# Routed experts: blocks numbered expert by expert, one fetch of each weight, a block table in registers, a split float32r down product

## The chip, the cores and the metric

One core of a Trainium2 chip runs the whole kernel. The metric is the device time of one execution in microseconds. The kernel before was run three times: median 1275.41 us, lowest 1274.18, highest 1277.51. A further execution was recorded by the hardware profiler.

## The reference

One layer of an encoder on 1024 tokens of width 1024: RMSNorm, one combined input projection, attention and a gated convolution in parallel, an output projection, and then a mixture of experts. The change touches only the last:

```
x = x + HierMoE(rms_norm(x, g_ffn))
# per token: the group of 8 experts with the highest logit, in it the two best experts
a = h @ w_e_gate[e];  u = h @ w_e_up[e]        # 1024 x 256 each, 32 experts
mid = silu(a) * u * weight(token, e)
x += mid @ w_e_down[e]                          # 256 x 1024
```

All of it is float32. An expert has 3 MB of weights, gate, up and down with 1 MB each. Each token goes to two experts, so 2048 rows are spread over 32 experts.

## The kernel before

Each engine has its own program (`block.sync` for SyncE's queue, `block.gpsimd`, `block.scalar` for ACT, `block.vector`, `block.tensor`), and semaphores tie them together. The stages are the input projection, attention, the two branches with their merge, the output projection with routing, and the expert stage.

Routing gives every (token, expert) pair a place in a list of blocks of 128 rows. Each of the 32 experts has a home block with its own number (`home`), and rows past the 128th go into overflow blocks from number 32 on (`shift`, `over`, lines 1113 to 1122). `bexp` says which expert an overflow block belongs to, and `ntrip_i` how many groups of four there are, at least one (lines 1174 to 1181).

The expert stage runs over the blocks in groups of four (`SLOTS`), a hardware loop over groups and an unrolled body of four on every engine, and the last group behind the loop. A matrix product in full float32 precision is done as three float32r products (`three`, line 1219): the high part times the high part, low times high, high times low. The high part is a copy into a float32r tile, the low part is the difference of the two.

For a block, by engine:

- SyncE, `load_expert` (line 408): waits until the gate and up products of the block four before are done (`gu_ps`), issues gate and up weights into `wgu_raw`, waits for that block's down product (`y_ps`), issues `wed`. The overflow blocks load their expert's weights again, with the expert's number read from `bexp` into a register (lines 439 to 443).
- GpSimd: `gather` (line 531) fetches 128 rows by an indirect DMA into `hg`, five blocks ahead; `scatter` (line 539) adds the block's output rows to the result in DRAM by an indirect DMA and waits for the scatter before it to have landed (`y_out`).
- ACT, `act_block` (line 788): silu of the block, the high half of the weights of the block after the next in two pieces (`expert_hi`, 128x2048 each, lines 769 to 771), between them the high part of its gathered rows (`gathered_hi`), then the left half of the output (line 799).
- VectorE, `dve_block` (line 1191): silu times up (`mid`), the copy of the transposed product (`midT`), the low halves of the weights (`expert_lo`, line 1163, written over the raw tile) around the low part of the gathered rows (`gathered_lo`), the row indices and weights of the block (`rcol`, `wcol`), the right half of the output (line 1206).
- TensorE, `pe_block` (line 1506): half the gate and up product of the next block, transposes of `mid`, transposes of the gathered rows of the block after it, the other half, then `down` (lines 1495 to 1504): four float32 matmuls of 512 columns, two instructions each in the trace.

## Time and profile before

| | |
|---|---|
| median of three runs | 1275.41 us |
| profiled execution, whole | 1278.19 us |
| its span, first to last instruction | 1276.2 us |
| TensorE busy | 1171.4 us, 92% |
| VectorE busy | 756.7 us, 59% |
| ACT busy | 468.3 us, 37% |
| GpSimd busy | 199.4 us, 16% |
| expert weights fetched | 36 x 3 loads of 1024 KB |
| moved by all DMA | 172.26 MB, of it 16.81 MB by the indirect ones of GpSimd |
| expert stage, first weight load issued to the end | 817.3 to 1276.2 us |

Times in the rows are microseconds from the first instruction unless marked ns, and in rows a number in square brackets is the idle time of the engine before the instruction, with what ended it. L1163 is line 1163 of the kernel. PE is TensorE, PEld its weight loads, DVE VectorE, POOL GpSimd, SP SyncE, and a q behind a name its instruction queue. Matmul instructions overlap, so what one costs is the distance between two starts, and not the length shown.

### The profile page before, as it was taken

What the parts mean: (1) busy time and instruction counts of PE and PEld (TensorE: products, weight loads), DVE (VectorE), ACT (ScalarE), POOL (GpSimd) and SP (SyncE); (2) the same over time, 40 slices, a digit from 0 to 9 for tenths busy, and PEclk for the clock granted to TensorE, in tenths of its full rate; (3) what the DMA queues carried; (4) which work ended last, traced back from release to release, by engine and by line L of the source; (5) the groups of instructions that cost most, each with busy time, mean ns of one, the idle gap of its engine ahead of it and who ended that gap; (6) DMA issues with size and microseconds to landing.
All of it is one profiled execution on the core that took longest, in us unless ns stands there. A gap on an engine that the chain in (4) does not pass through costs nothing.

```text
span 1276.2 us, 14857 instructions
## 1 busy us (share of the span) xinstructions
PE 1171.4 (92%) x5388; PEld 891.4 (70%) x5388; DVE 756.7 (59%) x992; ACT 468.3 (37%) x635; POOL 199.4 (16%) x243
## 2 busy tenths in 40 slices
PE   4999999999878999999999899859999889889996
PEld 4988888886645576776778788746676656666664
DVE  4448999983424454544465334476777556556663
ACT  4522111113533444444232111124555544554552
POOL 4010000000232332120000000011222221222121
PEclk9999999999969999999799899858999999999999
DMA  6021111111000000000410323495999999999980
GB/s 224 1 66 33 49 49 49 50 50 34 24 1 1 1 1 1 1 17 18 164 56 11 96 107 132 171 318 165 327 337 319 305 323 313 343 328 311 313 279 9
DMA packets 101541, 172.26 MB, mean 135 GB/s; under 512 B 11727, under 2 KB 45690, under 8 KB 101498
## 3 DMA queue, kind: packets, MB, share of 16 engines
q1 hardware_dynamic: 91002, 154.86, 35.8%
q0 software_dynamic: 10432, 16.81, 5.5%
q8 instruction: 26, 0.43, 0.1%
q14 instruction: 17, 0.14, 0.0%
q10 hardware_dynamic: 64, 0.02, 0.0%
HBM read 165.35 MB, written 27.26 MB: 151 GB/s over the span
## 4 chain that ended last, share of the span: by engine, by line
PE 67%; DMA 13%; DVE 6%; ACT 5%; issue 5%; SPq 2%; POOL 2%; ACTq 0%; DVEq 0%; POOLq 0%
PE pb L1221 14%; PE pb L1223 14%; PE pb L1222 14%; DMA wgu_raw<-in_w_e_up 11%; PE pb L1503 5%; PE pb L1361 4%; PE pb L1338 4%; PE pb L1350 2%; PE pb L1270 2%; PE pb L1475 2%; PE pb L1280 1%; SPq L417 1%; PE pb L1421 1%; DMA ws_raw<-in_w_conv_out 1%; ACT wgu_hi L771 1%
## 5 line engine op out<-in xcount | busy, mean ns | idle before, releaser
L1163 DVE TENSOR_TENSOR wgu_lo<-wgu_raw,wgu_hi 128x2048 fp32r<-128x2048 f32 x72 | 164.6, 2287 | 63.5 <-ACT wgu_hi L771 63.4
L771 ACT ACTIVATE wgu_hi<-wgu_raw 128x2048 fp32r<-128x2048 f32 x72 | 137.1, 1908 | 56.5 <-DMA wgu_raw<-in_w_e_up 56.5
L871 DVE SCALAR_TENSOR_TENSOR cv<-up,dwc,cv 128x1024 f32<-128x1024 f32 x120 | 154.1, 1284 | 3.7
L1221 PE MATMUL pb<-hT_hi,ws_hi 128*128 128x512 f32 x384 | 151.7, 395 | 0.0
L1223 PE MATMUL pb<-hT_hi,ws_lo 128*128 128x512 f32 x384 | 149.5, 389 | 0.0
L1222 PE MATMUL pb<-hT_lo,ws_hi 128*128 128x512 f32 x384 | 149.5, 389 | 0.0
L1221 PE MATMUL pb<-wgu_hi,hgT_hi 128*128 128x512 f32 x288 | 128.2, 445 | 6.3 <-DVE hgT_lo L1170 6.1
L1503 PE MATMUL pb<-wed,midT 128*128 128x512 f32 x288 | 129.5, 592 | 0.5 <-DVE midT L1196 0.5
L1223 PE MATMUL pb<-wgu_hi,hgT_lo 128*128 128x512 f32 x288 | 113.7, 395 | 0.0
L1222 PE MATMUL pb<-wgu_lo,hgT_hi 128*128 128x512 f32 x288 | 113.3, 393 | 0.0
L1503 PEld LDWEIGHTS pb<-wed,midT 128*128 128x128 f32 x288 | 54.4, 189 | 55.2 <-issue 51.8
L694 ACT ACTIVATE pr<-pb,nmax 128x128 f32<-128x128 f32 (+7 forms) x64 | 47.4, 741 | 112.6 <-DVE nmax L989 112.6
L1221 PEld LDWEIGHTS pb<-hT_hi,ws_hi 128*128 128x128 f32 x384 | 72.1, 188 | 15.9 <-issue 1.0
L1222 PEld LDWEIGHTS pb<-hT_lo,ws_hi 128*128 128x128 f32 x384 | 72.1, 188 | 15.9 <-issue 1.0
L1361 PEld LDWEIGHTS pb<-vv,pT 128*128 128x128 f32 x576 | 73.1, 197 | 14.3 <-DVE pT L1005 7.5
L1223 PEld LDWEIGHTS pb<-hT_hi,ws_lo 128*128 128x128 f32 x384 | 72.1, 188 | 15.2
L1361 PE MATMUL pb<-vv,pT 128*128 128x64 f32 x576 | 75.4, 277 | 6.9 <-DVE pT L1005 6.3
L548 POOL DMA_INDIRECT out<-yb,rcol x36 | 57.4, 1595 | 151.5 <-issue 102.6
L1221 PEld LDWEIGHTS pb<-wgu_hi,hgT_hi 128*128 128x128 f32 x288 | 55.7, 193 | 28.9 <-issue 19.2
L1338 PE MATMUL pb<-kT,qT 96*128 96x512 f32 (+3 forms) x192 | 75.0, 500 | 0.5 <-DVE kT L938 0.5
L1005 DVE COPY pT<-pb 128x512 f32<-128x512 f32 (+3 forms) x64 | 37.7, 589 | 60.5 <-PE pb L1350 60.2
L799 ACT ACTIVATE yb<-pb,wcol 128x512 f32<-128x512 f32 x36 | 24.8, 690 | 125.8 <-DVE wcol L1203 67.8
(281 smaller groups left out, 2017.8 us busy)
## 6 DMA issues: line engine op xcount, KB each, us to landing
wgu_raw<-in_w_e_gate SPq DMA_DIRECT2D x36, 1024.0 KB, 11.2
wgu_raw<-in_w_e_up SPq DMA_DIRECT2D x36, 1024.0 KB, 20.6
wed<-in_w_e_down SPq DMA_DIRECT2D x36, 1024.0 KB, 18.4
ws_raw<-in_w_in SPq DMA_DIRECT2D x24, 512.0 KB, 3.8
xs<-in_x SPq DMA_DIRECT2D x8, 512.0 KB, 8.7
wout<-in_w_out SPq DMA_DIRECT2D x1, 4096.0 KB, 12.8
xb<-in_x SPq DMA_DIRECT2D x8, 512.0 KB, 5.2
h_rows<-h SPq DMA_DIRECT2D x8, 512.0 KB, 2.6
```

Source lines behind the costliest of these rows:

```text
L548: g.indirect_dma_start(out=out[0], out_offset=bass.IndirectOffsetOnAxis(ap=rcol[b][:, 0:1].bitcast(U32), axis=0), in_=yb[b][:, :], in_offs ...
L694: a.activation(pr[:, n % 2, 0:w], banks(2 * (n % 2), 2)[:, 0:w], ACT.Exp, bias=nmax[:, n % 2:n % 2 + 1], accum_out=rsum[:, j % 2, h:h + 1] ...
L771: a.activation(wgu_hi[q % 2][:, :, ks, :], wgu_raw[q % SLOTS][:, :, ks, :], ACT.Copy).then_inc(gu_hi, 1)
L871: i = v.scalar_tensor_tensor(out=cv[:, c, :], in0=src, scalar=w, in1=cv[:, c, :], op0=ALU.mult, op1=ALU.add)
L1005: v.tensor_copy(pT[:, m % 2, 0:min(512, (j + 1) * P)], banks(4, 1)[:, 0:min(512, (j + 1) * P)]).then_inc(pt_d, 1)
L1163: v.tensor_tensor(wgu_lo[q % SLOTS][:, :, ks, :], wgu_raw[q % SLOTS][:, :, ks, :], wgu_hi[q % 2][:, :, ks, :].bitcast(F32), ALU.subtract). ...
L1221: t_.matmul(out, w(0), m(0), start=start, stop=False)
L1222: t_.matmul(out, w(0), m(1), start=False, stop=False)
L1223: return t_.matmul(out, w(1), m(0), start=False, stop=stop)
L1338: t_.matmul(S[:, f:e], qT[0:QK, j % 2, h * P:(h + 1) * P], kT[0:QK, h, f:e], start=True, stop=(e < w))
L1361: i = t_.matmul(pb[:, 6, h * VD:(h + 1) * VD], pT[:, n % 2, k * P:(k + 1) * P], vv[:, k, h * VD:(h + 1) * VD], start=(k == 0), stop=(k == j))
L1503: m = t_.matmul(pb[:, 4 + h, :], midT[:, f, :], wed[q][:, f, h * 512:(h + 1) * 512], start=(f == 0), stop=(f == 1))
```

## The change

- Blocks are numbered expert by expert: the blocks of expert 0, then those of expert 1, and so on, at least one each. The total is rounded up to a multiple of four.
- SyncE's program no longer has loops: it fetches each expert's weights once, in order, gate and up into one of four places of `wgu_raw`, down into one of three places of `wed_raw`. It waits for a register's value of `gu_lo` and `dn2_lo` (`landed_by`: twice the number of blocks up to that expert) before it fills a place again, and counts landed weights in `gu_here` and `down_here`, in program order.
- A table `btab_i` holds for each block its expert's number plus one, the place of its gate and up weights, and the place of its down weights. VectorE computes it, TensorE turns it into one row, and ACT, VectorE and GpSimd read its entries into registers.
- The low halves of gate and up weights have two tiles of their own, so that the raw tile stays.
- The down product is split in the same way as the gate and up product, 12 float32r matmuls a block: ACT copies the high part of the down weights (`down_hi`, two halves of 128x1024), GpSimd subtracts for the low part (`down_lo`), VectorE splits `midT`.
- ACT and VectorE do their steps in a new order: silu and `mid` of the next block come before the output of this one, and the first half of the weights is split three blocks ahead.

```diff
 SLOTS = 4
+DSLOTS = 3
 NBT = MAXB + SLOTS
+NTAB = 64
 GLU_UNITS = 2 * NC
 GATE_UNITS = 2 * D // P
...
-    WO = [R2 + 24 * K * i for i in range(SLOTS)]
-    wgu_raw = [place(f"wgu_raw{i}", [P, 2, KD, FF], F32, o) for i, o in enumerate(WO)]
-    wgu_lo = [place(f"wgu_lo{i}", [P, 2, KD, FF], F32R, o) for i, o in enumerate(WO)]
+    wgu_raw = place("wgu_raw", [P, SLOTS, 2, KD, FF], F32, R2)
+    wed_raw = place("wed_raw", [P, DSLOTS, 2, D], F32, R3)
     wgu_hi = [place(f"wgu_hi{i}", [P, 2, KD, FF], F32R, R1 + 16 * K * i) for i in range(2)]
-    wed = [place(f"wed{i}", [P, 2, D], F32, o + 16 * K) for i, o in enumerate(WO)]
+    wgu_lo = [place(f"wgu_lo{i}", [P, 2, KD, FF], F32R, o) for i, o in enumerate((R1 + 32 * K, R6 + 8 * K))]
+    wed_hi = place("wed_hi", [P, 2, D], F32R, R6)
+    wed_lo = place("wed_lo", [P, 2, D], F32R, R3 + 24 * K)
...
+    sil = place("sil", [P, FF], F32, ONO)
+    mid = place("mid", [P, FF], F32, ONO + K)
+    midT = [place(f"midT_{n}", [P, 2, P], F32R, QDO + 8 * K + K * s) for s, n in enumerate(("hi", "lo"))]
...
+            pair = "(o p i) f -> p o (i f)"
+            def load_gu(e):
+                b = e % SLOTS
+                sp.dma_start(wgu_raw[:, b, 0, :, :].rearrange("p (o i) f -> p o (i f)", i=2), w_e_gate[0, e].rearrange(pair, p=P, i=2)).then_inc(w_in0[b], 16)
+                sp.dma_start(wgu_raw[:, b, 1, :, :].rearrange("p (o i) f -> p o (i f)", i=2), w_e_up[0, e].rearrange(pair, p=P, i=2)).then_inc(w_in0[b], 16)
+            def load_down(e):
+                b = e % DSLOTS
+                sp.dma_start(wed_raw[:, b, :, :], w_e_down[0, e].rearrange("(k p) f -> p k f", p=P)).then_inc(w_in1[b], 16)
+            def confirm_gu(e):
+                sp.wait_ge(w_in0[e % SLOTS], 32 * (e // SLOTS + 1))
+                sp.sem_inc(gu_here, 1)
+            def confirm_down(e):
+                sp.wait_ge(w_in1[e % DSLOTS], 16 * (e // DSLOTS + 1))
+                sp.sem_inc(down_here, 1)
...
-                    load_expert(0, 0, None)
+                    load_gu(0)
...
+            for e in range(1, SLOTS):
+                load_gu(e)
+                load_down(e - 1)
+            confirm_gu(0)
             sp.wait_ge(bexp_ok, 1)
...
-                    load_expert(q, e, i * SLOTS + (q + 1 + NE - SLOTS))
+            for e in range(SLOTS, NE + 2):
+                confirm_gu(e - 3)
+                if e >= SLOTS + 1:
+                    confirm_down(e - SLOTS - 1)
+                if e < NE:
+                    split = sp.value_load(landed_by[0:1, e - SLOTS:e - SLOTS + 1], min_val=2, max_val=2 * MAXB)
+                    sp.wait_ge(gu_lo, split)
+                    load_gu(e)
+                if e >= SLOTS + 1:
+                    split = sp.value_load(landed_by[0:1, e - SLOTS - 1:e - SLOTS], min_val=2, max_val=2 * MAXB)
+                    sp.wait_ge(dn2_lo, split)
+                    load_down(e - 2)
+            confirm_gu(NE - 1)
+            for e in range(NE - 3, NE):
+                confirm_down(e)
             sp.wait_ge(y_all, 2)
...
+            def table(col):
+                return btab_i[0:1, bass.ds(col, 1)]
+            def down_lo(q, i):
+                s = pool.value_load(table(i * SLOTS + (q + 2 * NTAB)), min_val=0, max_val=DSLOTS - 1)
+                for h in range(2):
+                    pool.wait_ge(dn2_hi, i * (2 * SLOTS) + (2 * q + h + 1))
+                    g.tensor_tensor(wed_lo[:, h, :], wed_raw[:, bass.ds(s, 1), h, :].rearrange("p o f -> p (o f)"), wed_hi[:, h, :].bitcast(F32), ALU.subtract).then_inc(dn2_lo, 1)
...
+            down_lo(0, 0)
             with pool.Fori(0, last) as i:
                 for q in range(SLOTS):
                     gather(q % 2, i * SLOTS + (q + SLOTS + 1))
+                    down_lo(q + 1, i)
                     scatter(q % 2, i * SLOTS + (q + 1), i * (8 * SLOTS) + 16 * ((q + 1) // 2 + 1))
             for q in range(SLOTS):
+                if q < SLOTS - 1:
+                    down_lo(q + 1, last)
                 scatter(q % 2, last * SLOTS + (q + 1), last * (8 * SLOTS) + 16 * ((q + 1) // 2 + 1))
...
+            def expert_hi(q, h, s):
                 ks = slice(h * (KD // 2), (h + 1) * (KD // 2))
-                a.activation(wgu_hi[q % 2][:, :, ks, :], wgu_raw[q % SLOTS][:, :, ks, :], ACT.Copy).then_inc(gu_hi, 1)
+                raw = wgu_raw[:, 0, :, ks, :] if s is None else wgu_raw[:, bass.ds(s, 1), :, ks, :].rearrange("p o g k f -> p (o g) k f")
+                a.activation(wgu_hi[q % 2][:, :, ks, :], raw, ACT.Copy).then_inc(gu_hi, 1)
+            def place_of(q, i):
+                return act.value_load(table(i * SLOTS + (q + NTAB)), min_val=0, max_val=SLOTS - 1)
+            def first_half(q, i):
+                e = act.value_load(table(i * SLOTS + q), min_val=1, max_val=NE)
+                s = place_of(q, i)
+                act.wait_ge(gu_here, e)
+                expert_hi(q, 0, s)
+            def down_hi(q, i):
+                e = act.value_load(table(i * SLOTS + q), min_val=1, max_val=NE)
+                s = act.value_load(table(i * SLOTS + (q + 2 * NTAB)), min_val=0, max_val=DSLOTS - 1)
+                act.wait_ge(down_here, e)
+                act.wait_ge(y_ps, i * SLOTS + (q + 1))
+                for h in range(2):
+                    a.activation(wed_hi[:, h, :], wed_raw[:, bass.ds(s, 1), h, :].rearrange("p o f -> p (o f)"), ACT.Copy).then_inc(dn2_hi, 1)
+            def silu(q, i):
+                nth = i * SLOTS + (q + 1)
+                act.wait_ge(gu_ps, nth)
+                a.activation(sil[:, :], pb[:, GU_BANK[q % 2], 0:FF], ACT.Silu).then_inc(sil_ok, 1)
...
+            act.wait_ge(gu_here, 1)
+            expert_hi(0, 0, None)
+            expert_hi(0, 1, None)
             act.wait_ge(bexp_ok, 1)
-            last = act.value_load(ntrip_i[0:1, 1:2], min_val=NE // SLOTS, max_val=MAXB // SLOTS - 1)
-
-            def act_block(q, i, more):
+            first_half(1, 0)
+            gathered_hi(0, 1)
+            expert_hi(1, 1, place_of(1, 0))
+            gathered_hi(1, 2)
+            last = act.value_load(ntrip_i[0:1, 0:1], min_val=NE // SLOTS - 1, max_val=MAXB // SLOTS - 1)
+            act.wait_ge(swt_ps, 1)
...
+            def act_block(q, i, left):
                 nth = i * SLOTS + (q + 1)
-                act.wait_ge(gu_ps, nth)
-                a.activation(sil[:, :], pb[:, GU_BANK[q % 2], 0:FF], ACT.Silu).then_inc(sil_ok, 1)
-                if more:
-                    act.wait_ge(w_in0[(q + 2) % SLOTS], (i + (q + 2) // SLOTS) * 32 + 32)
-                    expert_hi(q + 2, 0)
+                if left > 2:
+                    expert_hi(q + 2, 1, place_of(q + 2, i))
                     gathered_hi(q, i * SLOTS + (q + 3))
-                    expert_hi(q + 2, 1)
-                act.wait_ge(y_ps, nth)
+                if left > 1:
+                    silu(q + 1, i)
+                if left > 3:
+                    first_half(q + 3, i)
+                if left > 1:
+                    down_hi(q + 1, i)
+                act.wait_ge(y_ps, nth + 1)
                 act.wait_ge(wc_ok, nth)
                 a.activation(yb[q % 2][:, 0:512], pb[:, 4, :], ACT.Copy, scale=wcol[q % 2][:, :]).then_inc(y_a, 1)
+            silu(0, 0)
+            first_half(2, 0)
+            down_hi(0, 0)
             with act.Fori(0, last) as i:
                 for q in range(SLOTS):
-                    act_block(q, i, True)
+                    act_block(q, i, SLOTS)
             for q in range(SLOTS):
-                act_block(q, last, q < SLOTS - 2)
+                act_block(q, last, SLOTS - q)
...
-            link(v.tensor_scalar(shift[:, :], shift[:, :], float(P), float((NE - 1) * P), ALU.mult, ALU.add))
-            link(v.tensor_tensor(shift[:, :], shift[:, :], home[:, :], ALU.subtract))
-            v.tensor_tensor(rank[:, :, :], ranks, row(home[:, :], NE), ALU.add)
-            link(v.scalar_tensor_tensor(out=over[:, :, :], in0=ranks, scalar=float(P), in1=row(shift[:, :], NE), op0=ALU.is_ge, op1=ALU.mult))
-            link(v.tensor_tensor(rank[:, :, :], rank[:, :, :], over[:, :, :], ALU.add))
+            link(v.scalar_tensor_tensor(out=shift[:, :], in0=shift[:, :], scalar=float(P), in1=home[:, :], op0=ALU.mult, op1=ALU.add))
+            link(v.tensor_tensor(rank[:, :, :], ranks, row(shift[:, :], NE), ALU.add))
...
+            link(v.tensor_tensor(incl[:, :], incl[:, :], up32[:, :], ALU.add))
+            link(v.tensor_scalar(bcmp[:, :], incl[:, :], pcol[:, 0:1], None, ALU.is_le))
+            link(v.reduce_sum(be_f[:, 0:1], bcmp[:, :], axis=AX.X))
+            link(v.tensor_scalar(be_f[:, 1:2], be_f[:, 0:1], float(NE - 1), None, ALU.min))
+            link(v.tensor_copy(be_i[:, 0:1], be_f[:, 1:2]))
+            v.tensor_scalar(btab[:, 0:1], be_f[:, 1:2], 1.0, None, ALU.add)
+            v.tensor_scalar(cmp3[:, :], io3[:, :], be_f[:, 1:2], None, ALU.is_le)
+            link(v.tensor_single_scalar(be_i[:, 1:2], be_i[:, 0:1], SLOTS - 1, op=ALU.bitwise_and))
+            link(v.reduce_sum(be_f[:, 0:1], cmp3[:, :], axis=AX.X))
+            v.tensor_copy(btab[:, 1:2], be_i[:, 1:2])
+            v.scalar_tensor_tensor(out=btab[:, 2:3], in0=be_f[:, 0:1], scalar=-float(DSLOTS), in1=be_f[:, 1:2], op0=ALU.mult, op1=ALU.add).then_inc(btab_ok, 1)
+            v.tensor_scalar(landed_by[:, :], incl[0:1, :], 2.0, None, ALU.mult)
+            link(v.tensor_scalar(cmp4[:, :], io4[:, :], incl[0:1, NE - 1:NE], None, ALU.is_lt))
+            link(v.reduce_sum(ntrip_f[:, :], cmp4[:, :], axis=AX.X))
+            v.tensor_scalar(ntrip_i[:, :], ntrip_f[:, :], -1.0, None, ALU.add)
...
-            def expert_lo(q, h, halves):
+            dve.wait_ge(btab_ps, 1)
+            v.tensor_copy(btab_i[:, :], pb[0:1, 5, 0:3 * NTAB]).then_inc(bexp_ok, 1)
+            def table(col):
+                return btab_i[0:1, bass.ds(col, 1)]
+            def expert_lo(q, h, i):
                 ks = slice(h * (KD // 2), (h + 1) * (KD // 2))
-                dve.wait_ge(gu_hi, halves)
-                v.tensor_tensor(wgu_lo[q % SLOTS][:, :, ks, :], wgu_raw[q % SLOTS][:, :, ks, :], wgu_hi[q % 2][:, :, ks, :].bitcast(F32), ALU.subtract).then_inc(gu_lo, 1)
+                s = dve.value_load(table(i * SLOTS + (q + NTAB)), min_val=0, max_val=SLOTS - 1)
+                dve.wait_ge(gu_hi, i * (2 * SLOTS) + (2 * q + h + 1))
+                v.tensor_tensor(wgu_lo[q % 2][:, :, ks, :], wgu_raw[:, bass.ds(s, 1), :, ks, :].rearrange("p o g k f -> p (o g) k f"), wgu_hi[q % 2][:, :, ks, :].bitcast(F32), ALU.subtract).then_inc(gu_lo, 1)
...
-            expert_lo(0, 0, 1)
-            expert_lo(0, 1, 2)
...
+            for i in range(2):
+                dve.wait_ge(h2_out[i], 16 * NTILE // 2)
+            dve.wait_ge(bexp_ok, 1)
+            last = dve.value_load(ntrip_i[0:1, 0:1], min_val=NE // SLOTS - 1, max_val=MAXB // SLOTS - 1)
+            expert_lo(0, 0, 0)
+            expert_lo(0, 1, 0)
             dve.wait_ge(swt_ps, 1)
...
+            expert_lo(1, 1, 0)
+            def middle(q, i):
+                nth = i * SLOTS + (q + 1)
+                dve.wait_ge(sil_ok, nth)
...
+            def dve_block(q, i, left):
                 b, nth = q % 2, i * SLOTS + (q + 1)
-                dve.wait_ge(sil_ok, nth)
-                v.tensor_tensor(mid[:, :], sil[:, :], pb[:, GU_BANK[b], FF:2 * FF], ALU.mult).then_inc(mid_ok, 1)
+                m = pb[:, 3, 0:FF].rearrange("p (f t) -> p f t", f=2)
                 dve.wait_ge(mt_ps, nth)
-                v.tensor_copy(midT[:, :, :], pb[:, 3, 0:FF].rearrange("p (f t) -> p f t", f=2)).then_inc(mt_ok, 1)
-                if more:
-                    expert_lo(q + 2, 0, i * (2 * SLOTS) + (2 * q + 5))
+                v.tensor_copy(midT[0][:, :, :], m).then_inc(mt_hi, 1)
+                dve.wait_ge(mt_hi, nth)
+                v.tensor_tensor(midT[1][:, :, :], m, midT[0][:, :, :].bitcast(F32), ALU.subtract).then_inc(mt_ok, 1)
+                if left > 2:
+                    expert_lo(q + 2, 1, i)
                     gathered_lo(b, i * SLOTS + (q + 3), i * SLOTS + (q + SLOTS))
-                    expert_lo(q + 2, 1, i * (2 * SLOTS) + (2 * q + 6))
+                if left > 1:
+                    middle(q + 1, i)
                 dve.wait_ge(y_out[b], i * (8 * SLOTS) + 16 * (q // 2 + 1))
                 v.tensor_scalar(rcol[b][:, :], stok[:, bass.ds(i * SLOTS + q, 1)], 0.0, None, ALU.add)
                 v.tensor_scalar(wcol[b][:, :], swt[:, bass.ds(i * SLOTS + q, 1)], 1.0, None, ALU.mult).then_inc(wc_ok, 1)
+                if left > 3:
+                    expert_lo(q + 3, 0, i)
                 dve.wait_ge(wc_ok, nth)
-                dve.wait_ge(y_ps, nth)
+                dve.wait_ge(y_ps, nth + 1)
                 v.tensor_scalar(yb[b][:, 512:1024], pb[:, 5, :], wcol[b][:, :], None, ALU.mult).then_inc(y_d_ok, 1)
+            middle(0, 0)
+            expert_lo(2, 0, 0)
             with dve.Fori(0, last) as i:
                 for q in range(SLOTS):
-                    dve_block(q, i, True)
+                    dve_block(q, i, SLOTS)
             for q in range(SLOTS):
-                dve_block(q, last, q < SLOTS - 2)
+                dve_block(q, last, SLOTS - q)
...
+            pe.wait_ge(btab_ok, 1)
+            for c in range(3):
+                i = t_.matmul(pb[0:1, 5, c * NTAB:(c + 1) * NTAB], btab[:, c:c + 1], ident[:, 0:NTAB], start=True, stop=True)
+            i.then_inc(btab_ps, 1)
...
+            pe.sem_inc(y_ps, 1)
...
-                    m = three(pb[:, GU_BANK[q % 2], :], lambda s: hgT[q % 2][s][:, k, :], lambda s: (wgu_lo[q % SLOTS] if s else wgu_hi[q % 2])[:, :, k, :], k == 0, k == KD - 1)
+                    m = three(pb[:, GU_BANK[q % 2], :], lambda s: hgT[q % 2][s][:, k, :], lambda s: (wgu_lo if s else wgu_hi)[q % 2][:, :, k, :], k == 0, k == KD - 1)
...
-                pe.wait_ge(w_in1[q], i * 16 + 16)
+                pe.wait_ge(dn2_lo, i * (2 * SLOTS) + (2 * q + 2))
...
-                        m = t_.matmul(pb[:, 4 + h, :], midT[:, f, :], wed[q][:, f, h * 512:(h + 1) * 512], start=(f == 0), stop=(f == 1))
+                        m = three(pb[:, 4 + h, :], lambda s: midT[s][:, f, :], lambda s: (wed_lo if s else wed_hi)[:, f, h * 512:(h + 1) * 512], f == 0, f == 1)
```

## Rows read from the trace of the kernel before

**Rows 1.** The page's part 1: busy us by engine (share of the span) x instructions

```profile
PE 1171.4 (92%) x5388; PEld 891.4 (70%) x5388; DVE 756.7 (59%) x992; ACT 468.3 (37%) x635; POOL 199.4 (16%) x243
```

**Rows 2.** Stages: length, PE, PEld, DVE, ACT, POOL busy, clock, DMA share, GB/s

```profile
935.00:955.00 20.00, 20.00 (x85) 14.17 (x84) 14.73 (x18) 11.19 (x10) 5.27 (x4) 1.00 0.99 330
1050.00:1100.00 50.00, 44.73 (x177) 31.18 (x178) 30.42 (x38) 25.19 (x22) 11.78 (x9) 0.95 0.99 327
1100.00:1150.00 50.00, 46.50 (x187) 32.34 (x187) 31.71 (x37) 26.44 (x24) 10.55 (x8) 0.98 1.02 330
```

**Rows 3.** The chain of waits, early blocks: start, us, what

```profile
881.32 3.43 PE pb L1503 x8
...
891.43 3.43 PE pb L1503 x8
```

**Rows 4.** The same chain, later blocks

```profile
1056.14 3.45 PE pb L1503 x8
...
1067.09 20.52 DMA wgu_raw<-in_w_e_up
...
1096.19 1.28 ACT L791
...
1104.07 3.45 PE pb L1503 x8
```

**Rows 5.** The same chain, the end

```profile
1261.89 0.69 ACT yb L799
...
1264.32 3.71 PE pb L1503 x8
...
1269.90 1.55 POOL out L548
```

**Rows 6.** Groups of instructions, 850 to 1276: busy us, mean ns, idle before

```profile
L1163 DVE TENSOR_TENSOR wgu_lo<-wgu_raw,wgu_hi 128x2048 fp32r<-128x2048 f32 x72 | 164.6, 2287 | 63.5 <-ACT wgu_hi L771 63.4
L771 ACT ACTIVATE wgu_hi<-wgu_raw 128x2048 fp32r<-128x2048 f32 x68 | 129.8, 1908 | 56.5 <-DMA wgu_raw<-in_w_e_up 56.5
...
L1170 DVE TENSOR_TENSOR hgT_lo<-pb,hgT_hi 128x1024 fp32r<-128x1024 f32 x36 | 43.7, 1215 | 1.8 <-ACT hgT_hi L775 1.8
...
L1196 DVE COPY midT<-pb 128x256 f32<-128x256 f32 x36 | 15.3, 424 | 34.4 <-PE pb L1492 34.4
```

**Rows 7.** DMA issues: KB each, median us from issue to landing

```profile
wgu_raw<-in_w_e_up SPq DMA_DIRECT2D x36, 1024.0 KB, 20.6
```

**Rows 8.** TensorE in order of time, gate-up products

```profile
919.73 0.40 PE L1223 MATMUL pb<-wgu_hi,hgT_lo 128*128 128x512 f32 x1
919.96 0.40 PE L1221 MATMUL pb<-wgu_hi,hgT_hi 128*128 128x512 f32 x1
```

**Rows 9.** SyncE's queue in order of time

```profile
884.78 0.37 SPq L417 DMA_DIRECT2D wed<-in_w_e_down  x1
...
1163.02 4.76 SPq L417 DMA_DIRECT2D wed<-in_w_e_down  x1
1168.03 3.74 SPq L413 DMA_DIRECT2D wgu_raw<-in_w_e_gate  x1
...
1210.02 3.41 SPq L417 DMA_DIRECT2D wed<-in_w_e_down  x1
...
1214.35 2.10 SPq L413 DMA_DIRECT2D wgu_raw<-in_w_e_gate  x1
```

**Rows 10.** VectorE and GpSimd in order of time, first 60 us

```profile
18.79 2.33 DVE L856 TENSOR_TENSOR wdn_lo<-wdn_raw,wdn_hi 128x2080 fp32r<-128x2080 f32 x1 [1.64 <-ACT wdn_hi L603]
...
18.84 4.96 POOL L493 TENSOR_TENSOR wdn_lo<-wdn_raw,wdn_hi 128x1248 fp32r<-128x1248 f32 x1 [3.98 <-ACT wdn_hi L603]
23.88 0.19 POOL L485 TENSOR_SCALAR rs<-ss 128x1 f32<-128x1 f32 x1
...
24.79 0.75 POOL L485 TENSOR_SCALAR rs<-ss 128x1 f32<-128x1 f32 x1
```

**Rows 11.** VectorE in order of time, the wait for the slot product

```profile
852.91 0.21 DVE L1154 TENSOR_SCALAR stok<-pb 128x52 int32<-128x52 f32 x1 [3.04 <-PE pb L1457]
```

80 lines of the change are left out of this document (27 added, 53 removed).

## The prediction

> **What bounds the kernel now.** Read the engine totals first [rows 1]: TensorE is 92% busy over the span, but that is an average. The change touches only the expert stage, the last third, so I read the busy times by stage next [rows 2]. At 935 to 955 TensorE is busy without a gap and the DMA share is already 0.99; at 1050 to 1150 TensorE drops to 44.7 and 46.5 of 50 us while the DMA share stays at 0.99 and 1.02. The chain shows both regimes. Early, it is pure TensorE work and a block costs 10.12 us (the down products start at 881.32 and 891.43) [rows 3]. Later it is issue by SyncE, 20.52 us of landing, then ACT and VectorE halves, and four blocks cost 47.93 us, 11.98 each (1056.14 to 1104.07) [rows 4]. Over the stage, first down end to last down end is 884.75 to 1268.03, 383.3 us for 35 intervals, 10.95 each [rows 3, 5]. So two things hold the stage: TensorE at 10.1 us a block, and weight traffic of 36 x 3 MB.
>
> The other engines have room now. Scaled from 20 us at 935 to 955 to a block of 10.12 us, VectorE is busy 14.73 / 20 x 10.12 = 7.5 us a block, of it 2 x 2.29 with the weights' low halves and 1.21 with the gathered rows'; ACT 11.19 gives 5.7 us, of it 2 x 1.91 with the high halves; GpSimd, which only issues a gather and a scatter, 5.27 gives 2.7 us [rows 2, 6].
>
> **The change part by part.**
> Number of blocks: counted from the reference's router on these inputs, experts 18, 19, 20 and 22 of the 32 get 129 to 256 rows and all others 1 to 128, so 32 + 4 = 36 blocks, as the trace has: 36 loads of each weight [rows 6, 7]. Rounded up to a multiple of four it is 36 before and after. Nothing is gained in blocks.
>
> DMA: 36 x 3 MB become 32 x 3 MB, 12.6 MB less; at the 330 GB/s of the saturated stretches [rows 2] that is 38 us of DMA time. It is worth that only where DMA is the bound. The after kernel also frees a raw slot when VectorE has taken its low half, not when TensorE has used it, so a load starts earlier than before by about 2 blocks less the 12.5 us at which the low half is done, some 8 us. With the four overflow blocks in the middle (blocks 19 to 26), where no load is needed, I take DMA to be off the path from there on. In the first 18 blocks it needs 3.15 MB of weights + some 0.4 MB of rows per block over 0.33 MB/us = 10.8 us.
>
> Down products: 8 instructions in 3.43 us [rows 3] become 12 of the gate-up's form, which follow each other at 0.23 us [rows 8]: 2.74 us, 0.69 us less. TensorE then needs 10.12 - 0.69 = 9.43 us a block.
>
> ACT: adds two copies of 128x1024, half of the 1.91 us of 128x2048 each [rows 6], 1.9 us: 7.6 us. It also reads registers: SyncE's gap between two issues is 0.25 us in the loop without a read (1163.02 + 4.76 to 1168.03) and 0.92 us with one (1210.02 + 3.41 to 1214.35) [rows 9], so 0.67 us each. Of ACT's five reads a block two stand behind the short silu and cost about 1.1 us, the others lie under running copies. That makes 8.7 us, still under 9.4. VectorE: one more 128x256, 0.42 us as the `midT` copy [rows 6]: 7.9 us.
>
> GpSimd: the new low halves of 128x1024. The only row of this form is 128x1248 in 4.96 us, started together with VectorE's 2.33 us on the same two tiles, one engine's instruction held by the other's: 4.96 - 2.33 = 2.63 us for 1248, so 2.15 us for 1024; one short GpSimd form tells the same, 0.75 us where it meets a running VectorE instruction and 0.19 where not [rows 10]. Bounds for one half: 1.15 us (VectorE's 2.29 for 2048 halved; the ring below falls to 8.8 and TensorE's 9.43 holds) and 4.1 us (4.96 scaled, always held). I take 2.15 when free, the value of its own row less the hold, and price the hold by the order of work; 4.1 would count it twice, so it sets no end of the range. GpSimd's sum is 4.3 + 2.7 = 7.0 us. The Trainium skill, "SBUF — State Buffer", section "Who interferes with whom", speaks against this part: a VectorE instruction with two SBUF inputs and a GpSimd one that reads SBUF exclude each other for their whole length, whichever began first. The trace shows GpSimd waiting for VectorE; no row shows VectorE waiting for GpSimd. By the rule the forecast below stands; without it the first rival.
>
> So I price the exclusion in both directions. No engine's sum exceeds 9.4 us, but the order does. From the end of gate-up n+1 (time 0): silu to 0.6, reads, ACT's first high half of n+3 from 1.65 to 3.55, the two down copies to 5.45, output copy, second high half to 8.0. VectorE's low half of n+3 runs 3.6 to 5.85 and holds off GpSimd, which takes 5.85 to 8.0; at 8.0 VectorE's next low half and GpSimd's second become ready together. If GpSimd is first, the ring is VectorE half 2.29, gathered low half 1.21, `mid` 0.42, the two short column instructions 0.3, GpSimd half 2.15, VectorE half 2.29, GpSimd half 2.15: 10.8 us a block. If VectorE is first, the down product starts at 12.6 and the next one on time, (12.6 + 9.43) / 2 = 11.0. I take 10.8.
>
> New wait on SyncE: weights e are reported as landed (gu_here) only after the down load of e is issued, which waits for the down low half of e-3. Behind that wait are queued the report, ACT's high half of e, and behind it the down copies of e-2: a ring of 1.9 + 2.3 + 2.15 + 2.15 + 0.3 = 8.8 us plus the issue. An issue takes 0.37 us with an empty queue and 3 to 4 us with a full one [rows 9]. At 10.8 us a block the queue is not full for long, so I price it at nothing; its cover is the 2.0 us between 8.8 and 10.8.
>
> Start: the table takes 15 small VectorE instructions of some 0.2 us, 3 us, ahead of the wait for the slot product, in which VectorE sat idle for 3.04 us [rows 11]; three longer ones ahead of it and eight behind it go. If that cover were gone, the stage would begin 3 us later. The first low halves come as before. The first down product must wait for copies and two GpSimd halves behind the third block's low half: 3 us later, end 887.7 instead of 884.7. End: the last block's down copies and GpSimd halves follow the down product before, 1.0 + 4.3 + 0.3 + 2.9 = 8.5 us instead of the present 6.1 (1261.9 to 1268.0), then 8.1 us as now [rows 5].
>
> Sum: 887.7 + 34 x 10.8 + 8.5 + 8.1 = 1271.5 us of span. The profiled execution had a span of 1276.2 and 1278.19 us in all, the median of the runs is 1275.41, 0.8 under the span. So 1271 us.
>
> **The rivals.**
> 1. The exclusion works only against GpSimd, or costs little. Then GpSimd's halves overlap VectorE's and a block costs 9.4 to 10.0; the first 18 stay at DMA's 10.6. 887.7 + 18 x 10.6 + 16 x 9.9 + 16.6 = 1253.5; with 9.43 in the second part 1246. For it: no row shows VectorE held. Against it: the two tiles' reads that hold GpSimd are the same.
> 2. Slower: the report behind the down load. From an issue time of 2.0 us on, SyncE's ring exceeds 10.8; at 3.5 us it is 12.3. In the 18 blocks where DMA is nearly full that is + 27 us: 1298. For it: the share of 0.99 already at 10.1 us a block, and landings of 20.6 us [rows 2, 7]. Against it: 12.6 MB less, and earlier loads.
> 3. Slower: reads and ties fall badly (each read on ACT's path over 1 us, VectorE first at most ties, ACT's table load of 1.28 us each fourth block [rows 4]): 11.4 us, 1271 + 34 x 0.6 = 1291.
> 4. The loads aren't saved: only if an expert were empty or the count differed; the 36 blocks speak against it. It would read as 36 loads and some 1290.
>
> **How the numbers follow.** Forecast 0.40 (1262 to 1280, from 10.55 to 11.05 a block); rival 1 0.26; rival 2 0.20; rival 3 0.12; rival 4 0.02. Within 0.3% (about what a measurement of this kernel can tell from no change) is 1271.6 to 1279.2. Faster: rival 1 and 0.21 of the forecast, 0.47. Same: 0.13 of the forecast and 0.02 of the others, 0.15. Slower: 0.38. The forecast alone straddles the line. Range 1240 to 1303: below, rival 1 with 9.43; above, rival 2 with a margin for its 18 blocks becoming 20.
>
> **What would show it.** 32 loads of each weight. Down products of 12 at 0.23 us. GpSimd's halves near 2.15 us where VectorE is idle and up to 4.4 beside it; VectorE's 2.29 us stretched in turn (mean over 2.6) is the exclusion, unchanged 2.29 is rival 1. Down starts 10.8 us apart. TensorE's waits moved from landings to the down low half and hgT_lo. ACT's high half waiting for SyncE after a long down issue is rival 2. The prediction is wrong if the distance of the down starts is under 10.4 or over 11.2.

## The result and the profile after

The kernel after the change takes 1310.47 us (median of four runs, 1310.02 to 1314.04); the kernel before, on the same chip, 1275.96. The ratio is 1.0277, with a 95% interval of 1.0254 to 1.0300: slower by 2.8%. The forecast was 1271 us and its range ended at 1303. The profiled execution has a span of 1307.7 us and took 1310.24 us. Ratios here and below are of undisturbed executions: one of the four of experiment 7 took 2347.45 us, nearly double, is left out of its ratio, and why it did so is open.

Two lines of the page of the kernel after: the engine totals and the loads of the up weights (median us to landing at the end). They answer to [rows 1, 7].

```profile
PE 1165.0 (89%) x5538; PEld 923.2 (71%) x5538; DVE 833.6 (64%) x1034; ACT 531.0 (41%) x701; POOL 468.4 (36%) x319
...
wgu_raw<-in_w_e_up SPq DMA_DIRECT2D x32, 1024.0 KB, 11.8
```

Two engines changed out of proportion. GpSimd went from 199 to 468 us, and VectorE gained 77 us although only some 36 x 0.42 us, 15 us, of work of its own was added in the blocks. The loads are 32 instead of 36 and land in 11.8 us, where they took 20.6.

Stages of the kernel after: length, then busy us of PE, PEld, DVE, ACT and POOL, granted clock, DMA share, GB/s [rows 2].

```profile
880.00:1050.00 170.00, 147.45 (x647) 117.93 (x646) 121.15 (x144) 107.80 (x100) 140.67 (x57) 0.92 0.83 283
1050.00:1240.00 190.00, 161.63 (x748) 125.66 (x748) 173.04 (x163) 124.77 (x114) 173.08 (x66) 1.00 0.78 251
```

TensorE is busy for 87 and 85%, also where the DMA share is only 0.78. The transfers no longer set the pace there; in the second stretch VectorE and GpSimd are both at 91%.

Groups of the kernel after, 850 us to the end: busy us, mean ns of one, then the idle time before and its releasers [rows 6].

```profile
L1262 DVE TENSOR_TENSOR wgu_lo<-wgu_raw,wgu_hi 128x2048 fp32r<-128x2048 f32 x72 | 232.0, 3224 | 52.8 <-ACT wgu_hi L820 50.5 <-issue 1.8
L591 POOL TENSOR_TENSOR wed_lo<-wed_raw,wed_hi 128x1024 fp32r<-128x1024 f32 x72 | 199.2, 2787 | 40.9 <-ACT wed_hi L837 40.3
L580 POOL DMA_INDIRECT out<-yb,rcol x36 | 97.0, 2693 | 19.1 <-issue 11.8 <-DMA out<-yb,rcol 6.9
L567 POOL DMA_INDIRECT hg<-h_rows,icol x36 | 70.2, 1949 | 33.5 <-issue 25.9 <-DVE icol L1267 7.6
```

The same VectorE instruction had a mean of 2287 ns before [rows 6]; it is the same instruction on the same shape and takes 0.94 us more on average. The stretching shows in a single block. GpSimd of the kernel after, in order of time (start, us, what; in brackets the idle time before):

```profile
1104.60 4.73 POOL L591 TENSOR_TENSOR wed_lo<-wed_raw,wed_hi 128x1024 fp32r<-128x1024 f32 x2
1109.49 3.47 POOL L580 DMA_INDIRECT out<-yb,rcol  x1 [0.17 <-issue]
1113.27 2.98 POOL L567 DMA_INDIRECT hg<-h_rows,icol  x1 [0.30 <-issue]
1116.27 4.74 POOL L591 TENSOR_TENSOR wed_lo<-wed_raw,wed_hi 128x1024 fp32r<-128x1024 f32 x2
```

And VectorE in the same 12 us:

```profile
1105.73 5.75 DVE L1262 TENSOR_TENSOR wgu_lo<-wgu_raw,wgu_hi 128x2048 fp32r<-128x2048 f32 x1 [0.42 <-ACT wgu_hi L820]
1111.41 0.14 DVE L1267 TENSOR_SCALAR icol<-stok 128x1 int32 x1
1111.47 1.21 DVE L1269 TENSOR_TENSOR hgT_lo<-pb,hgT_hi 128x1024 fp32r<-128x1024 f32 x1
1112.60 0.40 DVE L1287 TENSOR_TENSOR mid<-sil,pb 128x256 f32<-128x256 f32 x1
...
1113.05 2.28 DVE L1262 TENSOR_TENSOR wgu_lo<-wgu_raw,wgu_hi 128x2048 fp32r<-128x2048 f32 x1
1115.25 0.74 DVE L1308 TENSOR_SCALAR yb<-pb,wcol 128x512 f32<-128x512 f32 x1
```

Read the two side by side. VectorE's half begins at 1105.73, while GpSimd's halves run until 1109.33, and ends only at 1111.48: 2.29 us of work after a hold of 3.46. The scatter issued at 1109.49 takes 3.47 us, not 1.6: it waits for that VectorE half to end and then does its work. The gather issued at 1113.27 takes 2.98 us, not 1.04: it waits for VectorE's second half, until 1115.33. That second half itself is not held (2.28 us). So each of the two engines waits for the other in turn, and GpSimd has no idle time in this block but the gaps of 0.17 and 0.30 us. The closed ring of one block is GpSimd's halves 4.73, rest of VectorE's half 2.08, small VectorE work 1.64, second half 2.28, rest of the gather 0.92, 0.02 to the next halves: 11.67 us.

The scatter is not in this ring. In 5 of the 17 blocks between 1050 and 1240 it began 1.0 to 2.2 us late, because it waits for the scatter before it to have landed, and then took 1.60 to 2.64 us. Those blocks are 11.66 to 11.69 us long all the same, since the gather behind it is held until VectorE's second half ends. The landing of the scatters, which the chain of waits often names in this stretch, is therefore not what makes a block longer.

### The profile page after: what moved, and what is told of

Same layout as the page of the kernel before. It is cut to its first block, busy times and chain, and to the rows that moved or that the text cites. A ratio compares the mean times of both kernels' runs of the same rounds, so it can differ in the third digit from the quotient of the medians.

```text
span 1307.7 us, 16802 instructions
## 1 busy us (share of the span) xinstructions
PE 1165.0 (89%) x5538; PEld 923.2 (71%) x5538; DVE 833.6 (64%) x1034; ACT 531.0 (41%) x701; POOL 468.4 (36%) x319
## 4 chain that ended last, share of the span: by engine, by line
PE 63%; issue 9%; DVE 7%; DMA 7%; POOL 5%; ACT 5%; DVEq 1%; ACTq 1%; SPq 1%; POOLq 0%
PE pb L1325 15%; PE pb L1327 14%; PE pb L1326 14%; DMA out<-yb,rcol 6%; PE pb L1465 4%; PE pb L1442 4%; POOL wed_lo L591 3%; PE pb L1454 2%; PE pb L1374 2%; PE pb L1384 1%; DVE wgu_lo L1262 1%; PE pb L1525 1%; DVE hgT_lo L1269 1%; DMA ws_raw<-in_w_conv_out 1%; PE pb L1584 1%
## 5 line engine op out<-in xcount | busy, mean ns | idle before, releaser
L1262 DVE TENSOR_TENSOR wgu_lo<-wgu_raw,wgu_hi 128x2048 fp32r<-128x2048 f32 x72 | 232.0, 3224 | 52.8 <-ACT wgu_hi L820 50.5
L591 POOL TENSOR_TENSOR wed_lo<-wed_raw,wed_hi 128x1024 fp32r<-128x1024 f32 x72 | 199.2, 2787 | 40.9 <-ACT wed_hi L837 40.3
L820 ACT ACTIVATE wgu_hi<-wgu_raw 128x2048 fp32r (+1 forms) x72 | 137.4, 1910 | 63.1 <-SPq L432 35.3
L517 POOL TENSOR_SCALAR ssh<-ssh 128x8 f32<-128x8 f32 x16 | 3.1, 196 | 403.6 <-DVE ssh L1008 402.8
L1325 PE MATMUL pb<-wgu_hi,hgT_hi 128*128 128x512 f32 x288 | 119.8, 416 | 8.5 <-DVE hgT_lo L1269 8.5
L1325 PE MATMUL pb<-wed_hi,midT_hi 128*128 128x512 f32 x144 | 64.2, 446 | 55.0 <-issue 29.2
L517 POOL TENSOR_SCALAR rs<-ss 128x1 f32<-128x1 f32 x16 | 3.8, 236 | 284.9 <-ACT sq L804 261.5
L580 POOL DMA_INDIRECT out<-yb,rcol x36 | 97.0, 2693 | 19.1 <-issue 11.8
L837 ACT ACTIVATE wed_hi<-wed_raw 128x1024 fp32r x72 | 72.2, 1051 | 47.7 <-PE pb L1327 38.3
L1465 PEld LDWEIGHTS pb<-vv,pT 128*128 128x128 f32 x576 | 73.1, 198 | 14.3 <-DVE pT L1083 7.5
L567 POOL DMA_INDIRECT hg<-h_rows,icol x36 | 70.2, 1949 | 33.5 <-issue 25.9
## 6 DMA issues: line engine op xcount, KB each, us to landing
wgu_raw<-in_w_e_up SPq DMA_DIRECT2D x32, 1024.0 KB, 11.8
```

The source lines that it names most:

```text
L567: g.indirect_dma_start(out=hg[b][:, :], out_offset=None, in_=h2_d, in_offset=bass.IndirectOffsetOnAxis(ap=icol[b][:, 0:1].bitcast(U32), ax ...
L580: g.indirect_dma_start(out=out[0], out_offset=bass.IndirectOffsetOnAxis(ap=rcol[b][:, 0:1].bitcast(U32), axis=0), in_=yb[b][:, :], in_offs ...
L591: g.tensor_tensor(wed_lo[:, h, :], wed_raw[:, bass.ds(s, 1), h, :].rearrange("p o f -> p (o f)"), wed_hi[:, h, :].bitcast(F32), ALU.subtra ...
L820: a.activation(wgu_hi[q % 2][:, :, ks, :], raw, ACT.Copy).then_inc(gu_hi, 1)
L837: a.activation(wed_hi[:, h, :], wed_raw[:, bass.ds(s, 1), h, :].rearrange("p o f -> p (o f)"), ACT.Copy).then_inc(dn2_hi, 1)
L1262: v.tensor_tensor(wgu_lo[q % 2][:, :, ks, :], wgu_raw[:, bass.ds(s, 1), :, ks, :].rearrange("p o g k f -> p (o g) k f"), wgu_hi[q % 2][:, ...
```

## The experiments

Each ratio is against the kernel before on the same chip, whose median lay between 1277.97 and 1278.92 us in the experiments. In the expectations, X is the theory that VectorE's and GpSimd's instructions with two SBUF inputs hold each other, in both directions, and that this and GpSimd's place in the order of a block make the kernel slow. S is rival 2, the report of landed weights queued behind the down load on SyncE. A is ACT's order with its register reads. Kernel 1 is the kernel of experiment 1, and so on.

**1. Take the low half away.** GpSimd still waits and still reports, but writes eight columns instead of 1024 in all blocks but the first, so the rest of the low half is left out:

```diff
-            def down_lo(q, i):
+            def down_lo(q, i, n=8):
...
-                    g.tensor_tensor(wed_lo[:, h, :], wed_raw[:, bass.ds(s, 1), h, :]..., wed_hi[:, h, :].bitcast(F32), ALU.subtract).then_inc(dn2_lo, 1)
+                    g.tensor_tensor(wed_lo[:, h, 0:n], wed_raw[:, bass.ds(s, 1), h, 0:n]..., wed_hi[:, h, 0:n].bitcast(F32), ALU.subtract).then_inc(dn2_lo, 1)
...
-            down_lo(0, 0)
+            down_lo(0, 0, D)
```

> The kernel after, but GpSimd subtracts the low half of the down weights for block 0 only; for all later blocks its two instructions cover 8 columns of 1024, so the down product uses a stale low half (that part of the computation is left out). Theory X, the exclusion between VectorE's two-input instructions and all GpSimd instructions (subtractions, and the issues of gather and scatter, which went from 1.6 and 1.1 us to 2.7 and 1.9 on average): without 4.8 us of subtraction GpSimd is far from full, VectorE's weight halves return to about 2.3 us and a block costs 9.6 to 10.3 us instead of 11.7; time 1245 to 1265 us. Theory S, SyncE's report behind the down load: the order of waits is as before, only the low half is done earlier; 1285 to 1300. Theory A, ACT's order with its register reads: about 10.8 us a block, 1275.

Measured: 1251.89 us, ratio 0.9789 (0.9772 to 0.9806). Its groups, 850 us to the end:

```profile
L1262 DVE TENSOR_TENSOR wgu_lo<-wgu_raw,wgu_hi 128x2048 fp32r<-128x2048 f32 x72 | 165.7, 2302 | 86.0 <-ACT wgu_hi L820 83.4 <-issue 2.4
```

All other parts of the change together are worth 2.1%; the GpSimd halves alone cost some 58 us, though GpSimd had the room for them by its sum. VectorE's half is back at its old length.

**2. The same low halves on VectorE**, behind its output instruction; nothing else moved:

```diff
+            def down_lo(q, i):
+                s = dve.value_load(table(i * SLOTS + (q + 2 * NTAB)), min_val=0, max_val=DSLOTS - 1)
+                for h in range(2):
+                    dve.wait_ge(dn2_hi, i * (2 * SLOTS) + (2 * q + h + 1))
+                    v.tensor_tensor(wed_lo[:, h, :], wed_raw[:, bass.ds(s, 1), h, :]..., wed_hi[:, h, :].bitcast(F32), ALU.subtract).then_inc(dn2_lo, 1)
```

> The kernel after with the two subtractions of the down weights' low half given to VectorE, at the end of its block, all else the same. Theory X: two instructions of about 1.2 us instead of 2.4 and nothing to exclude but the two DMA issues; VectorE's sum becomes 10.3 to 10.6 us a block and it is the bound, 10.6 to 11.0 us a block; time 1268 to 1285. Theory S or A: GpSimd wasn't the cause, and VectorE now has more to do: 1305 to 1325.

Measured: 1272.11 us, ratio 0.9954 (0.9938 to 0.9971). Groups and, below, the stretch of 1130 to 1230 of this kernel:

```profile
L1252 DVE TENSOR_TENSOR wgu_lo<-wgu_raw,wgu_hi 128x2048 fp32r<-128x2048 f32 x72 | 164.7, 2289 | 29.6 <-issue 17.2 <-ACT wgu_hi L810 12.3
L1278 DVE TENSOR_TENSOR wed_lo<-wed_raw,wed_hi 128x1024 fp32r<-128x1024 f32 x72 | 84.9, 1219 | 0.7 <-ACT wed_hi L827 0.5 <-issue 0.2
```

```profile
1130.00:1230.00 100.00, 93.04 (x441) 74.83 (x440) 94.77 (x118) 70.99 (x67) 27.74 (x19) 1.00 0.83 271
```

Work given to the engine with the larger sum is 38 us cheaper than on the one with room. One half costs VectorE 1.22 us and GpSimd 2.36 free. VectorE is 95% busy in this stretch, TensorE 93%, and VectorE is the likely bound.

**3. The report ahead of the down load.**

```diff
             for e in range(SLOTS, NE + 2):
-                confirm_gu(e - 3)
...
                     load_gu(e)
+                if e - 2 < NE:
+                    confirm_gu(e - 2)
```

> The kernel after with one change in SyncE's program: the landing of gate and up weights e-2 is reported right after the load of e is issued, ahead of the wait for the down low half, instead of behind the down load. Theory X: GpSimd's instructions and their holds fill its 11.7 us; within 0.5% of the kernel after, 1304 to 1314. Theory S: ACT waited 33 us in all for this report in 15 blocks; time 1275 to 1290.

Measured: 1310.74 us, ratio 1.0254 (1.0237 to 1.0272), against 1.0277 with the report behind. Rival 2 falls: ACT's high halves waited 32.9 us in all for this report in the kernel after and not at all here, and the time is the same. SyncE's queue fits that. In the kernel after an issue takes 0.4 to 0.7 us from 850 us on, never the 3 to 5 us of [rows 9]:

```profile
910.85 0.37 SPq L428 DMA_DIRECT2D wed_raw<-in_w_e_down  x1
911.98 0.37 SPq L423 DMA_DIRECT2D wgu_raw<-in_w_e_gate  x1
912.39 0.51 SPq L424 DMA_DIRECT2D wgu_raw<-in_w_e_up  x1
```

**4. The single fetch and the new numbering with the old float32 down product.** ACT's copy of the weight stays, so that the raw place comes free early; `wed_hi` and `midT` are plain float32 tiles, TensorE and SyncE wait for ACT's copy, and there is no low half of the down weights or of `midT`. The main line of the edit:

```diff
-                        m = three(pb[:, 4 + h, :], lambda s: midT[s][:, f, :], lambda s: (wed_lo if s else wed_hi)[:, f, h * 512:(h + 1) * 512], f == 0, f == 1)
+                        m = t_.matmul(pb[:, 4 + h, :], midT[0][:, f, :], wed_hi[:, f, h * 512:(h + 1) * 512], start=(f == 0), stop=(f == 1))
```

> Numbering by expert, one fetch of each weight and the table alone: the down product is four float32 matmuls as before, from a copy of the down weights that ACT makes; no low half, no GpSimd subtraction, midT copied once. Theory X: TensorE needs 10.1 us a block again and nothing else exceeds it; down ends 10.2 us apart, about 885 + 34 x 10.2 + 7 + 8 = 1247 of span; 1245 to 1258 us, faster than the kernel before by 1.4 to 2.4%. Theory S: the ring through SyncE, 1285 or more. If the single fetch were worth nothing: 1270 to 1276.

Measured: 1258.54 us, ratio 0.9844 (0.9827 to 0.9860). It leaves nothing of the computation out and is faster than the kernel before (1.6%) and the kernel after. Its chain of waits, and its stages:

```profile
1075.64 3.43 PE pb L1600 x8
...
1085.76 3.43 PE pb L1600 x8
...
1095.87 3.43 PE pb L1600 x8
```

```profile
890.00:960.00 70.00, 70.00 (x292) 49.47 (x291) 50.40 (x63) 51.43 (x48) 23.53 (x14) 1.00 0.99 337
960.00:1060.00 100.00, 92.13 (x376) 63.22 (x375) 64.42 (x82) 67.48 (x65) 24.59 (x18) 1.00 0.94 311
1060.00:1130.00 70.00, 70.00 (x292) 49.40 (x292) 49.84 (x63) 50.44 (x48) 18.94 (x14) 1.00 0.84 259
1130.00:1230.00 100.00, 100.00 (x418) 70.91 (x417) 73.07 (x90) 74.66 (x70) 27.89 (x18) 1.00 0.77 254
```

The blocks are 10.12 us apart where four of them cost 47.93 before [rows 4]. The transfers still cost something only at 960 to 1060, 8 us of TensorE's time. Against the kernel before this kernel gains about 20 us, where the single fetch saves 38 us of DMA time. The new order of steps on ACT and VectorE is in it as well, and no run has the single fetch alone, so the 20 us are the worth of these parts together.

**5. The report first, in kernel 4.** The edit of experiment 3 on kernel 4.

> e4 (single fetch, down product in float32) with the report of landed gate and up weights ahead of the wait for the down load, as in e3. In e4 TensorE runs at 10.11 us a block but for 965 to 1060, where the DMA queue is full, an issue of the down load takes 4 to 7 us and the report stands behind it; ACT waited 25 us for it. If that order is the cause (the second rival of the prediction, uncovered once GpSimd's work is gone): 1248 to 1254 us. If DMA itself is the bound in that stretch: ACT's wait moves to the landing and the time stays at 1256 to 1260.

Measured: 1259.70 us, ratio 0.9853 (0.9837 to 0.9870): no gain. Here the condition of rival 2 is met, since an issue of SyncE takes up to 6.9 us between 960 and 1060 in kernel 4. But with the report of the gate and up weights first, ACT waits for the report of the down weights instead: 14.3 us for the one and 27.4 for the other, against 25.3 and 0.8 in kernel 4.

**6. The report first, in kernel 1**, where nothing on GpSimd stands in the way.

> e1 (split down product, low half computed for block 0 only, so that part is left out) with the report first. TensorE needs 9.4 us a block; e1 lost 13 us of TensorE time at 960 to 1060. If the order of the report is the cause: 1236 to 1244 us. If DMA is the bound there: 1248 to 1253.

Measured: 1255.65 us, ratio 0.9834 (0.9813 to 0.9855), against 0.9789 without the edit. That is some 0.4% slower, the two intervals do not overlap, and the expectation (at most 1253 us) missed; why it is slower was not looked into. ACT's wait moves as before, from 47.5 us for the one report to 10.0 and 31.2 us for the two. Putting the gate and up report first helps none of these kernels; whether the reports as such cost something in kernels 1 and 4 is open.

**7. Only the exclusion.** In kernel 4, GpSimd gets two subtractions a block, at the place of the low halves, on a tile of its own that nobody uses or waits for:

```diff
+                    pool.wait_ge(dn2_hi, i * (2 * SLOTS) + (2 * q + h + 1))
...
+                    g.tensor_tensor(own[:, 1, :], own[:, 0, :], own[:, 0, :], ALU.subtract).then_inc(own_ok, 1)
```

> e4 with two GpSimd subtractions of 128x1024 a block at the place where the kernel after has its own, on a tile of their own that nothing else reads and nobody waits for. Theory X (exclusion in both directions): VectorE's weight halves rise from 2.29 us to a mean of 2.7 to 3.2, a block costs 10.6 to 11.7 us, time 1275 to 1305. If the price in the kernel after was the wait of the down product for the low half and no exclusion: GpSimd's 7.5 us a block are hidden under TensorE's 10.1, halves stay at 2.29 and the time at 1257 to 1261.

Measured: 1271.05 us, ratio 0.9945 (0.9925 to 0.9965), 12.5 us above kernel 4. The three executions that agree took 1266.87 (the profiled one), 1270.87 and 1271.22 us. The size was overestimated (1275 to 1305 expected), the direction was right. GpSimd in order of time:

```profile
1103.49 1.90 POOL L593 TENSOR_TENSOR own<-own 128x1024 f32<-128x1024 f32 x1
1105.57 3.73 POOL L593 TENSOR_TENSOR own<-own 128x1024 f32<-128x1024 f32 x1 [0.18 <-POOL own L593]
```

VectorE in order of time:

```profile
1104.99 2.56 DVE L1265 TENSOR_TENSOR wgu_lo<-wgu_raw,wgu_hi 128x2048 fp32r<-128x2048 f32 x1 [1.27 <-ACT wgu_hi L823]
1107.47 0.14 DVE L1270 TENSOR_SCALAR icol<-stok 128x1 int32 x1
1107.54 1.21 DVE L1272 TENSOR_TENSOR hgT_lo<-pb,hgT_hi 128x1024 fp32r<-128x1024 f32 x1
```

Both directions within 6 us: VectorE's half is held until GpSimd's first subtraction ends (1105.4), GpSimd's second until VectorE's half ends (1107.5). The tiles have nothing in common. From 1107.5 on, GpSimd runs at its own length beside `hgT_lo`, whose first input lies in PSUM.

**8. As much time on GpSimd and more, with writes only**: three memsets of 4.6 us together in place of the two subtractions.

> e4 with three GpSimd memsets a block (128x2048, 128x2048, 128x1024, some 4.8 us in sum) at the same place, in the tile of e7. They read nothing. Theory X, in the form that two-input reads are what is shared: VectorE's halves stay at 2.29 and the time at 1257 to 1262. If any GpSimd work of this length holds VectorE or delays gather and scatter: as e7, 1275 or more.

Measured: 1259.22 us, ratio 0.9850 (0.9834 to 0.9867), the time of kernel 4. Groups, 850 us to the end:

```profile
L1266 DVE TENSOR_TENSOR wgu_lo<-wgu_raw,wgu_hi 128x2048 fp32r<-128x2048 f32 x72 | 165.0, 2293 | 101.2 <-ACT wgu_hi L824 98.9 <-issue 2.2
L594 POOL MEMSET own<- 128x2048 f32 x72 | 130.7, 1815 | 49.4 <-ACT wed_hi L841 43.4 <-POOL own L594 5.5 <-issue 0.4
```

It is the reading by GpSimd that holds VectorE, not a busy GpSimd.

**9. The low halves replaced by memsets that the down product waits for**: the length of GpSimd's work and every wait as in the kernel after, without its reads.

> The kernel after with GpSimd's two subtractions a block replaced by three memsets of the low half tile (128x2048, 128x2048, 128x1024, some 4.6 us in sum), for which the down product and SyncE wait as before; the low half is zero, so that part of the computation is left out. It keeps the waits and GpSimd's length and takes away the reads. Theory X (what costs is the exclusion by two-input reads): VectorE's halves at 2.3 us, 9.7 to 10.2 us a block, 1250 to 1265 us. If the waiting of the down product for a GpSimd step of this length is what costs: as the kernel after, 1295 to 1310.

Measured: 1272.80 us, ratio 0.9962 (0.9948 to 0.9977); 1250 to 1265 was expected, a miss. GpSimd in order of time, two stretches:

```profile
999.05 1.83 POOL L595 MEMSET wed_lo<- 128x2048 f32 x1
1001.03 1.81 POOL L595 MEMSET wed_lo<- 128x2048 f32 x1 [0.15 <-POOL wed_lo L595]
1003.00 0.95 POOL L595 MEMSET wed_lo<- 128x1024 f32 x1 [0.15 <-POOL wed_lo L595]
1005.20 1.60 POOL L580 DMA_INDIRECT out<-yb,rcol  x1 [1.25 <-issue]
1007.11 2.75 POOL L567 DMA_INDIRECT hg<-h_rows,icol  x1 [0.30 <-issue]
1009.84 1.84 POOL L595 MEMSET wed_lo<- 128x2048 f32 x1
...
1125.28 1.04 POOL L567 DMA_INDIRECT hg<-h_rows,icol  x1 [0.30 <-issue]
1126.39 1.81 POOL L595 MEMSET wed_lo<- 128x2048 f32 x1
```

VectorE's halves are at 2293 ns and the memsets at their own length; still a block takes 10.8 us in the first stretch (999.05 to 1009.84). A hold makes it so, though GpSimd reads nothing in its memsets: the gather is held to 2.75 us by VectorE's half. ACT's first copy was done and the memset handed to GpSimd at 1008.5, but it began behind the gather, at 1009.84, and TensorE then waited 1.1 us before the down product. In the second stretch the gather takes its own 1.04 us, TensorE doesn't wait, and the down products start 9.7 and 9.5 us apart (1121.75, 1131.42, 1140.93). Over the stage they are 10.6 us apart.

So the loss has two parts. Kernel 1 to this one, 1252 to 1273, is GpSimd's work as a link of the path together with held gathers ahead of it: GpSimd's length alone fits, as the second stretch shows, and held gathers that nobody waits for cost nothing (experiment 8 has them at a mean of 1823 ns). From here to the kernel after, 1273 to 1310, is the two-input reading, with the halves of both engines and the scatters held. The two are not strictly separate: without the first, experiment 7 shows only 12.5 us for the second. No run takes away the gather's hold alone.

**10. A fourth place for down weights, in kernel 4**, so that down loads start one expert earlier (`DSLOTS = 4`, `load_down(e - 1)`).

> e4 with four places for down weights instead of three, so the down load of expert e is issued one turn earlier and not in the middle of the queue-full stretch. If the short lookahead of the down weights costs time at 965 to 1060: 1248 to 1255 us. If that stretch is bound by the DMA rate itself (share 0.94 in e4): 1257 to 1260.

Measured: 1258.01 us, ratio 0.9842 (0.9820 to 0.9864), the time of kernel 4. Neither an earlier report nor an earlier load fills the stretch of 960 to 1060. With its DMA share of 0.94, the rate of the transfers is a likely bound there; no run varied the rate itself.

**11. One half on each engine**: GpSimd the first, VectorE the second.

> The kernel after with the first of the two subtractions of the down low half on GpSimd and the second on VectorE, at the end of its block. If a block costs what the instructions that exclude each other sum to (in the kernel after 2 x 2.29 of VectorE + 2 x 2.37, 1.6 and 1.04 of GpSimd = 12.0, measured 11.7), then here 2 x 2.29 + 1.15 + 2.37 + 1.6 + 1.04 = 10.7 with some of it overlapped: 10.2 to 10.8 us a block, 1258 to 1280 us. If the price is the down product's wait for any GpSimd step behind ACT's copies, the exclusion being secondary: 1285 to 1300.

Measured: 1276.56 us, ratio 0.9986 (0.9966 to 1.0006), inside the 1258 to 1280 expected. Groups, 850 us to the end:

```profile
L591 POOL TENSOR_TENSOR wed_lo<-wed_raw,wed_hi 128x1024 fp32r<-128x1024 f32 x36 | 132.4, 3677 | 37.8 <-ACT wed_hi L837 36.8 <-issue 0.2
L1287 DVE TENSOR_TENSOR wed_lo<-wed_raw,wed_hi 128x1024 fp32r<-128x1024 f32 x36 | 99.2, 2755 | 2.8 <-ACT wed_hi L837 2.8
```

Sharing doesn't share: two halves that start together run one after the other. VectorE's takes 2.76 us instead of 1.22, and the whole is slower than with both on VectorE.

## Why the prediction was wrong

The mechanism was the forecast's own, exclusion in both directions; the time was outside its range because a block was sized too small. Its ring of 10.8 us had the wait of the gather's issue for VectorE at nothing and GpSimd's half too short, and only two ties in the order were looked at. The difference between 1271.5 and the 1307.7 us of span, piece by piece:

- **Start**: the first down product ended at 891.8, not at 887.7: 4.1 us. The first two low halves took 7.89 us, free they take 4.73, because two of VectorE's halves fell on them; and most of this first down product's instructions followed each other at 0.43 us, the clock's lower level, after TensorE had waited for them.
- **Blocks**: from there to the end of the last but one, at 1285.9, are 394.1 us for 34 intervals, 11.59 each and not 10.8: 26.9 us. This is the step that failed. The first 14 intervals, until 1053, are 11.9 us on average; the 17 from 1062.8 to 1261.1 are 11.67.
- **End**: the last down product ended 11.6 us after the one before, not 8.5: 3.1 us. Of this, 2.5 us are its twelve instructions at 0.43 us instead of 0.23. TensorE had waited 5.94 us for the low half, as it does in the second fence below. The tail of output and scatter took 10.3 us instead of 8.1: 2.2 us.

The sum is 36.3 us, within 0.1 us of the difference. Low halves before the first down product, in GpSimd's order of time:

```profile
878.91 7.89 POOL L591 TENSOR_TENSOR wed_lo<-wed_raw,wed_hi 128x1024 fp32r<-128x1024 f32 x2 [9.39 <-ACT wed_hi L837]
```

The last down product, in TensorE's order of time:

```profile
1292.18 0.76 PE L1325 MATMUL pb<-wed_hi,midT_hi 128*128 128x512 f32 x1 [5.94 <-POOL wed_lo L591]
1292.74 0.63 PE L1326 MATMUL pb<-wed_lo,midT_hi 128*128 128x512 f32 x1
1293.17 0.63 PE L1327 MATMUL pb<-wed_hi,midT_lo 128*128 128x512 f32 x1
```

Step by step:

- **Blocks and loads**: right. There are 36 blocks and 32 loads of each weight, and 159.7 MB moved instead of 172.3 (12.5 MB less).
- **DMA off the path behind the middle**: right, with a share of 0.78 from 1050 on. Before it, the 10.8 us a block of transfers never set the time in the kernel after, since the ring was longer.
- **Down product**: right where the clock is at its higher level: instructions follow at 0.23 us, and the last but one ran from 1283.05 to 1285.86, 2.8 us. Not foreseen was the lower level. Six down products between 910 and 1034, every second one, had most instructions 0.43 us apart after a wait of TensorE for the low half, and took 4.4 to 4.6 us instead of 2.9 (the granted clock was 0.72 at 934 to 940). They lie on the chain of waits, and by these figures make up an estimated 10 of the 26.9 us. The wait alone does not decide it: the down product at 1053.20 followed one of 2.76 us and ran at the higher level.
- **ACT and VectorE**: ACT's sum was right to within the gap of its reads (124.77 of 190 us busy, 7.7 us in 11.67). VectorE is 10.6 us busy a block between 1050 and 1240, of it 3.05 held on average: 7.6 of its own against 7.9.
- **GpSimd's low half**: mis-sized. It is 2.36 us free, not 2.15, 0.43 us a block, and both halves stand in the ring.
- **The exclusion**: right in direction and in place, wrong in extent. It was priced for the low halves alone. The issues of scatter and gather, 1.60 and 1.04 us each, were counted at their length in GpSimd's sum (7.0 us; 7.37 measured) and kept out of the ring, although they are held as well, by 1.87 and 1.94 us. With 0.47 us of gaps that fills GpSimd's block. The ring of the forecast put one GpSimd half on each side of VectorE's second one. The ring in the trace has both in one piece and the rest of the gather (0.92 us) between VectorE's second half and them; VectorE's three terms are 6.00 us together instead of 6.51. That is 10.81 + 0.43 + 0.94 - 0.51 = 11.67. The scatter's hold is not in it.
- **The order in a block**: only two ties were looked at. Until 1050 the ring of 11.67 us is not the one that runs (the gathers take 1.04 us there). The kernel alternates, as the next two fences show: GpSimd's halves take 7.86 us in one block and 4.76 in the next, and two blocks cost 23.7 us (VectorE's half of 3.61 us at 896.48 comes again at 920.22). The bound for one half, 4.1 us for always held, was left out as a hold counted twice; 7.86 for two shows that something near it happens in every other block.
- **Report on SyncE priced at nothing**: right. Experiment 3 moves the time by nothing that can be measured.

GpSimd of the kernel after, in order of time, two blocks of the alternating stretch:

```profile
902.96 7.86 POOL L591 TENSOR_TENSOR wed_lo<-wed_raw,wed_hi 128x1024 fp32r<-128x1024 f32 x2
910.99 1.61 POOL L580 DMA_INDIRECT out<-yb,rcol  x1 [0.17 <-issue]
912.90 1.03 POOL L567 DMA_INDIRECT hg<-h_rows,icol  x1 [0.30 <-issue]
916.91 4.76 POOL L591 TENSOR_TENSOR wed_lo<-wed_raw,wed_hi 128x1024 fp32r<-128x1024 f32 x2 [2.98 <-ACT wed_hi L837]
```

One of the long down products of this stretch, in TensorE's order of time:

```profile
934.59 0.50 PE L1325 MATMUL pb<-wed_hi,midT_hi 128*128 128x512 f32 x1 [2.49 <-POOL wed_lo L591]
...
935.47 0.63 PE L1325 MATMUL pb<-wed_hi,midT_hi 128*128 128x512 f32 x1
935.90 0.63 PE L1326 MATMUL pb<-wed_lo,midT_hi 128*128 128x512 f32 x1
```

The row that could have warned was in [rows 10]: if a 2.33 us VectorE instruction holds a GpSimd one, everything on GpSimd has to be put in the order of the block with its hold, the two issues too. The rule cited from the Trainium skill, "SBUF — State Buffer", section "Who interferes with whom", is borne out by experiments 7 and 8: two SBUF inputs on VectorE against a reading GpSimd, whichever began first, and no hold beside a memset.

**The rivals.** Rival 1 (one direction only) is refuted: 3224 ns a half after, 2769 in experiment 7, 2293 with memsets. Even without the hold on VectorE, its 9.4 to 10.0 us a block were not reached in experiment 9 (10.6 on average), since held gathers stood ahead of GpSimd's work on the path. Rival 2 is refuted by experiment 3. Rival 3 named the outcome, ties that fall badly, but its price of 11.4 us came from ACT's reads; ACT's wait is not what the ring consists of. Rival 4 is refuted by the 32 loads. The signal named for "wrong" was a distance of the down starts over 11.2 us, and it is 11.6.

Open: what holds 960 to 1060 in kernel 4, what the alternating stretch costs apart from the clock, and whether the issue of an indirect DMA is held through the index column that it reads or in another way.

## What to carry to other kernels

Price work for GpSimd in the order of a block and not by its free time: where VectorE's instructions with two SBUF inputs fill 40% of it, a GpSimd instruction that reads SBUF, and the issue of a gather or scatter, can be longer by most of a VectorE instruction (1.9 of 2.29 us here), and the reading ones hold VectorE in turn; memsets did neither. Six of the waits that this made for TensorE were followed by a lower granted clock, and so cost a second time. Where the low half is needed, the engine that is already fuller may be the cheaper one (1272 against 1310 us). A transfer saved is worth the part of it that a wait ends on: here at most 20 of 38 us.

## What the runs showed of the hardware that was not expected

- The issue of an indirect DMA on GpSimd is held by a running VectorE instruction with two SBUF inputs, scatter from 1.60 to 3.47 us and gather from 1.04 to 2.98. It does not hold VectorE: in experiment 9, with 36 gathers of a mean of 1948 ns, the mean of VectorE's halves is 2293 ns.
- `hgT_lo` on VectorE, one input in PSUM and one in SBUF, held nothing here: GpSimd's subtraction in experiment 7 and the scatter at 1109.49 both go on beside it.
- A GpSimd subtraction of 128x1024 takes 2.36 us free from two tiles into float32r and 1.90 from one tile read twice into float32; a memset of 128x2048 takes 1.82 and of 128x1024 0.95.
- TensorE's granted clock was 0.80 at 880 to 897 in the kernel after, which waited for its first low halves, and 1.00 there in the kernel before and in kernel 4, which did not.
